# Value products of the sparse attention stage two groups behind the turns, with two result banks and two turn banks

## What is computed

```python
def nsa_cmp_slc(q, q_pos, kc, vc, c_end, ksb, vsb, rel_bias):
    s_c = einsum(q, kc) * scale + head_bias(rel_bias, rel_c)      # compressed keys
    p_c = masked_softmax(s_c, rel_c >= 0);  o_c = p_c @ vc
    imp = p_c.sum(axis=2)                                         # importance of each block
    score = where(valid, imp + where(forced, FORCE_BONUS, 0.0), -1.0)
    _, idx = top_k(score, min(N_SEL, nsb))                        # 16 blocks of 64 keys
    s_s = einsum(q, ks) * scale + bias_s;  o_s = masked_softmax(s_s) @ vs
    return o_c, o_s
# nsa_window: the same over the last 512 keys -> o_w
o = gt[:, :, 0] * o_c + gt[:, :, 1] * o_s + gt[:, :, 2] * o_w
```

## Time and profile before

| | |
|---|---|
| median of 3 runs | 2830.69 us (2830.21 to 2832.34) |
| profiled execution | 2836.41 us |
| its span | 2834.7 us |
| busy PE, DVE, ACT, POOL | 2646.6, 1317.6, 854.3, 701.4 us |
| mean granted TensorE clock | 0.961 |

### The profile page before, as it was taken

The page is one execution under the profiler, slowest core; times in us unless marked ns, Lnnn a source line. Parts: engine busy times, 40 slices in busy tenths (PEclk is TensorE's granted clock), DMA queues, the critical chain, the costliest instruction groups (busy, mean ns, idle before and its releaser), DMA issues. The chain is left out here.

```text
span 2834.7 us, 52982 instructions
## 1 busy us (share of the span) xinstructions
PE 2646.6 (93%) x21938; PEld 2429.6 (86%) x21938; DVE 1317.6 (46%) x2309; ACT 854.3 (30%) x1604; POOL 701.4 (25%) x554
## 2 busy tenths in 40 slices
PE   8999999999789887788879999999999999999997
PEld 8998999989778764455559899988999999999996
DVE  6999989213234356455543353234333323323233
ACT  5333101123123324565552222135221121120222
POOL 2222212222234320211113424301422222222232
PEclk9999999999889887999889999999999999999998
DMA  5122353332476624434316551233111111111112
GB/s 185 48 66 68 99 105 91 92 98 68 139 245 216 214 90 176 133 110 155 115 59 213 150 184 60 75 134 135 47 44 47 50 46 45 45 45 45 45 45 69
DMA packets 149345, 290.33 MB, mean 102 GB/s; under 512 B 28356, under 2 KB 97160, under 8 KB 146354
## 3 DMA queue, kind: packets, MB, share of 16 engines
q1 hardware_dynamic: 137586, 255.49, 28.7%
q0 software_dynamic: 11520, 31.47, 3.5%
HBM read 245.94 MB, written 51.93 MB: 105 GB/s over the span
## 5 line engine op out<-in xcount | busy, mean ns | idle before, releaser
L147 POOL TENSOR_TENSOR mlp_w_low<-mlp_w_raw,mlp_w_high 128x1024 fp32r<-128x1024 f32 x72 | 173.7, 2412 | 649.3 <-ACT mlp_w_high L143 649.3
L371 PE MATMUL in_psum<-x_high,in_w_high 128*128 128x352 f32 x1416 | 266.1, 330 | 21.3 <-DVE x_low L566 11.3
L147 POOL TENSOR_TENSOR in_w_low<-in_w_raw,in_w_high 128x1024 fp32r<-128x1024 f32 x59 | 145.8, 2471 | 546.7 <-ACT in_w_high L143 546.7
L2775 PE MATMUL mlp_psum<-mlp_in,mlp_w_high 128*128 128x352 f32 x1536 | 264.9, 324 | 0.0
L143 ACT ACTIVATE mlp_w_high<-mlp_w_raw 128x1024 fp32r<-128x1024 f32 x72 | 76.4, 1061 | 621.5 <-PE mlp_psum L2775 621.5
L371 PEld LDWEIGHTS in_psum<-x_high,in_w_high 128*128 128x128 f32 x1416 | 236.9, 191 | 29.4 <-issue 15.0
L371 PE MATMUL in_psum<-x_low,in_w_high 128*128 128x352 f32 x1416 | 259.5, 325 | 0.0
L371 PE MATMUL in_psum<-x_high,in_w_low 128*128 128x352 f32 x1416 | 259.0, 324 | 0.0
L2775 PEld LDWEIGHTS mlp_psum<-mlp_in,mlp_w_high 128*128 128x128 f32 x1536 | 251.2, 189 | 0.2
L371 PEld LDWEIGHTS in_psum<-x_low,in_w_high 128*128 128x128 f32 x1416 | 235.4, 190 | 0.0
L371 PEld LDWEIGHTS in_psum<-x_high,in_w_low 128*128 128x128 f32 x1416 | 234.8, 189 | 0.0
(11 more groups left out here) (475 smaller groups left out, 4457.3 us busy)
## 6 DMA issues: line engine op xcount, KB each, us to landing
mlp_w_raw<-in_w_mlp SPq DMA_DIRECT2D x64, 512.0 KB, 3.6
in_w_raw<-in_w_in SPq DMA_DIRECT2D x59, 512.0 KB, 4.2
nsa_ring<-in_cache_slc SPq DMA_DIRECT2D x144, 128.0 KB, 4.0
gdnp_page_ring<-in_cache_cmp POOLq DMA_DIRECT2D x128, 128.0 KB, 4.8
gdnp_page_ring<-in_cache_cmp SPq DMA_DIRECT2D x128, 128.0 KB, 5.0
u_scratch<-stage SPq DMA_DIRECT2D x28, 528.0 KB, 5.3
nsa_ring<-in_cache_slc POOLq DMA_DIRECT2D x112, 128.0 KB, 4.0
aux<-u_scratch SPq DMA_DIRECT2D x24, 528.0 KB, 4.2
```

Of the source, the lines that this page charges most:

```text
L147: self.nc.gpsimd.tensor_tensor(self.low[:, i % 2, 0:k * P], self.raw[:, i % 2, 0:k * P], self.high[:, i % 2, 0:k * P].bitcast(F32), ALU.su ...
L371: return mm(psum[:, e % 2, n, 0:WN], w[:, i % 2, c * P:(c + 1) * P], a[:, c, n * WN:(n + 1) * WN], start=x == 0 and c == 0, stop=x == 2 an ...
L2775: return mm(psum[:, e % 2, n, 0:WN], w[:, i % 2, c * P:(c + 1) * P], a(c)[:, column(n)], start=x == 0 and c == 0, stop=x == 2 and c == CHU ...
```

## The change

Values run two groups behind the turns, and across items: after each turn of group G, PE values all groups up to G-2 (`values_up_to`). Groups are numbered through all items. At i = 6 and behind the last item the remaining ones are valued at once. The results of items alternate between banks 6 and 7 (two regions), and ACT copies a result after the copy of the group two behind the item's last (`keep_result`), but that of item 2 at the end of the item. Turned groups use two PSUM banks; `pt` keeps three slots. DVE's wait for its slot of `s_` asks for the turns of the old item, no longer for its values.

```diff
-    SLOTS, TBANKS, REGIONS, LAG = 4, 3, 4, 3
+    SLOTS, TSLOTS, TBANKS, REGIONS, LAG = 4, 3, 2, 2, 3
...
+    BEHIND = 2
+    place_of_group = [(i, k) for i in range(NI) for k in range(len(groups(i)))]
+    ends_item = {first_group[i + 1] - 1: i for i in range(NI)}
...
-        pt = S("probs_t", [P, TBANKS, 4, P])
+        pt = S("probs_t", [P, TSLOTS, 4, P])
...
-        O_BANK, M0, M1 = 7, 6, 7
-        region = lambda i: ps[:, O_BANK, i % REGIONS * P:(i % REGIONS + 1) * P]
+        O_BANK, M0, M1 = 6, 6, 7
+        region = lambda i: ps[:, O_BANK + i % REGIONS, 0:P]
...
-            def tail(i, step):
-                n = len(groups(i))
-                if step < n:
-                    turn(i, step)
-                if step >= 1:
-                    values(i, step - 1)
+            valued = [0]
+
+            def values_up_to(end):
+                while valued[0] < end:
+                    values(*place_of_group[valued[0]])
+                    valued[0] += 1
...
                 if i == RANKED:
+                    values_up_to(first_group[i - LAG])
                     pe.wait_ge(flags_ready, 1)
...
-                tailing = [(i - LAG, s) for s in range(len(groups(i - LAG)) + 1)] if i >= LAG else []
+                tailing = [(i - LAG, s) for s in range(len(groups(i - LAG)))] if i >= LAG else []
                 for which, (n, k) in merged(scoring, tailing):
-                    (tail if which else score)(n, k)
+                    if which:
+                        turn(n, k)
+                        values_up_to(first_group[n] + k + 1 - BEHIND)
+                    else:
+                        score(n, k)
+            values_up_to(first_group[NI])
...
                     next(exp_parts, None)
+                    if G - BEHIND in ends_item and ends_item[G - BEHIND] != RANKED - LAG - 1:
+                        keep_result(ends_item[G - BEHIND])
+                if i == RANKED - LAG - 1:
+                    keep_result(i)
                 for _ in exp_parts:
                     pass
+
+            def keep_result(i):
+                kind, n, tt = items[i]
                 act.wait_ge(o_mm, i + 1)
...
+            for G in range(first_group[NI], first_group[NI] + BEHIND):
+                if G - BEHIND in ends_item:
+                    keep_result(ends_item[G - BEHIND])
...
                 if i >= SLOTS:
-                    dve.wait_ge(o_mm, i - SLOTS + 1)
+                    dve.wait_ge(pt_mm, first_group[i - SLOTS + 1])
```

More of the change, by code:

```diff
@@ L1741, in values @@
                         for b in range(HB):
-                            last = mm(region(i)[strip(b), :], pt[:, G % TBANKS, j, strip(b)], ring[:, n % SETS, b, j, PAGE:2 * PAGE],
+                            last = mm(region(i)[strip(b), :], pt[:, G % TSLOTS, j, strip(b)], ring[:, n % SETS, b, j, PAGE:2 * PAGE],
                                       start=j == 0, stop=j == 3 and final)
@@ L1745, in values @@
                     x, hf, c = sets[n]
-                    last = mm(region(i), pt[0:NEW, G % TBANKS, 0, :], vn[:, hf, 0 if x == WIN else 1, :], start=False, stop=True)
+                    last = mm(region(i), pt[0:NEW, G % TSLOTS, 0, :], vn[:, hf, 0 if x == WIN else 1, :], start=False, stop=True)
                 else:
@@ L1752, in values @@
                             v = vc[0:w, dims] if x == CMP else vtok[:, 0 if x == SLC else 1, vb, dims]
-                            last = mm(region(i)[dims, :], v, pt[0:w, G % TBANKS, 2 * j + g, :], start=k == 0 and j == 0, stop=x == CMP)
+                            last = mm(region(i)[dims, :], v, pt[0:w, G % TSLOTS, 2 * j + g, :], start=k == 0 and j == 0, stop=x == CMP)
                 last.then_inc(o_mm if final else pv_mm, 1)
-            def tail(i, step):
-                n = len(groups(i))
-                if step < n:
-                    turn(i, step)
-                if step >= 1:
-                    values(i, step - 1)
+            valued = [0]
[3 more added lines that the diff above has]
+                    valued[0] += 1
             for c0, c1, b in ((0, BANK, 0), (BANK, NBIAS, 1)):
@@ L1857, in copies @@
                     act.wait_ge(pt_mm, G + 1)
[L1858 to L1861, removed]
+                    if G >= TSLOTS:
+                        old = max(m for m in range(NI) if first_group[m] <= G - TSLOTS)
+                        finished = G - TSLOTS == first_group[old + 1] - 1
+                        act.wait_ge(*((o_mm, old + 1) if finished else (pv_mm, G - TSLOTS - old + 1)))
                     if kind == SET:
@@ L1865, in copies @@
                         w, cols = (4 * (tt + 1), 2 * P) if group[0][0] == CMP else (P, 2 * P * len(group))
-                    act.activation(pt[0:w, G % TBANKS, :, :].rearrange("p a b -> p (a b)")[:, 0:cols], turn_bank(G)[0:w, 0:cols], ACT.Copy
+                    act.activation(pt[0:w, G % TSLOTS, :, :].rearrange("p a b -> p (a b)")[:, 0:cols], turn_bank(G)[0:w, 0:cols], ACT.Copy
                                    ).then_inc(pt_out, 1)
                     next(exp_parts, None)
+                    if G - BEHIND in ends_item and ends_item[G - BEHIND] != RANKED - LAG - 1:
+                        keep_result(ends_item[G - BEHIND])
+                if i == RANKED - LAG - 1:
+                    keep_result(i)
                 for _ in exp_parts:
                     pass
+            def keep_result(i):
+                kind, n, tt = items[i]
                 act.wait_ge(o_mm, i + 1)
```

## The result

The changed kernel takes 2865.8 us (median of four runs, 2856.7 to 2874.0) against 2831.5 us before (four runs); the ratio is 1.0114, interval 1.0089 to 1.0138. It is slower, 34 us by the medians. The forecast was 2851 us, range 2829 to 2870. The profiled execution took 2867.5 us with a span of 2865.8, 31.1 us above that of before.

What follows compares the result with a forecast made beforehand. PE bounds the sparse stage's item loop, with ring waits, copy waits and half clock. Copies -28, ring +42, clock +6 and banks +1 gave +21, taken as +20.5 on 2830.7: 2851 us, range 2829 to 2870.

Steps and rivals of the forecast that it cites:

- The ring's term: Sparse stage's item loop: later release of ring halves makes PE's waits grow from 15.4 to 57 us, +42 (+34 to +50).
- the clock: Sparse stage's item loop: half-clock episodes rise from ten to fourteen, costing 34 us against 24; +6 (-6 to +15).
- Copies: Sparse stage's item loop: PE's waits for ACT's copies of turned probabilities shrink, 28 us back (20 to 37).
- Score banks: Sparse stage's item loop: PE's 3.3 us of waits for score banks, counted only in the 37 us upper bound given back.
- Two banks of turns, two regions: Sparse stage: turn banks 0 to +2 us, result regions 0, at most +1, drain ahead of block masks +1; +1 summed.
- Rival B: Ring loads keep up, taking under 7 us; waits stay at 15, copies give 28 and clock 8: 2795 us; chance 0.13.
- Rival C: Even: ring waits grow by only 30 us, copy holes close entirely (-34), clock steady: 2826 to 2836 us; chance 0.08.
- Rival D: ACT's order still holds copies back: only 9 us come back, ring waits grow by 50: 2878 us; chance 0.03.

Runs made afterwards that it cites:

- set_at_once: Changed kernel, but PE values everything up to a set right after that set's turns, so the ring's half is released nearly where it was before: 2828.6 us, ratio 0.9986.
- late_results: Changed kernel with PE's old order (values one group behind inside an item), keeping late result copies, two result banks and two turn banks: 2844.1 us, ratio 1.0048.
- keys_first_old_spread: Changed kernel with separate loads of keys (released by scores) and values, scores and turns spread as in the kernel before: 2812.8 us, ratio 0.9937.
- after_short: Changed kernel with only one page of a set loaded each by SP and POOL from set 2 on (14 of 16 loads left out): 2803.0 us, ratio 0.9893.

## Why the prediction was right, step by step

The sign, the mechanism and the range held, and the measured 34 us lie above the 20.5 forecast. The ring's term, the largest, came out within 1 us. Two terms were too small: the clock by some 9 us, and the waits for DVE, which stood in no term and took 13. Copies gave 5 us more than forecast. So it is in part luck that the time lies inside the range: its upper end was made of longer ring waits (+50) and less back at the copies (20), not of a lateness of DVE that the prediction didn't see. One reading of the page was loose, without effect on the sums: PE's row is below 90% in slices 11, 12 and 14 too, ahead of the stage. By the prediction's own steps:

*1. Copy waits.* Forecast 28 us back of 37; measured 32.6. One more value product ahead and no wait for results close nearly all holes, and this is nearer the upper bound. Where the ring is out of the way the change gains only 18 and 15 us; part of the rest goes to DVE, step 4.

*2. Ring waits.* Forecast 57 us in fourteen places, 10 or more at set 4 and over 8 at set 15; measured 56.7 in 13, 13.0 and 8.4. The other counted shortfalls, counted / measured: set 2 2.8/2.7, 3 2.7/2.3, 5 6.5/4.8, 6 4.7/3.8, 8 3.7/1.6, 10 7.5/7.1, 11 4.0/2.1, 12 3.0/2.7, 14 1.9/1.9, 16 6.1/5.1, 17 1.5/1.2. The issue order and one load's length gave a table that the chip followed at every set but set 9, where 1.0 us was counted and none came. Without set 4 the counted shortfalls sum to 54.2 us and the waits to 43.7; that the total met the forecast of 57 is owed to a judgement between 49 and 60, and to set 4. There the prediction named head 2's load ahead on SP but gave it no price, and it costs 3 us in the changed kernel and over 6 in set_at_once.

The cited rule of the Trainium skill ("DMA: Bandwidth & Descriptors", Rules for kernel authors), to issue early and wait late, agrees with the trace: issued later, the same loads cost PE 56.7 us of waits in place of 15.4. The estimate from that page's fit, 6.8 us for a set's load, does not hold here. The page gives the fit for one DMA, and a set is 16 of them: the ring waits of the changed kernel ended 9.1 to 10.3 us behind the release, but for set 4's 13.0. With 26 and 4 us of shortfalls that estimate's sum is +1 and not -1, which changes nothing here.

*3. The clock.* Forecast +6 us with +15 as its bound; measured +17 by the episodes and +14.8 by PE's busy time. The prediction's list has eleven waits over 2.6 us, not twelve, so by its own count thirteen episodes were to come; fifteen came. Eleven of them begin inside a ring wait or less than 2 us behind one, as at 1186.3, and hold 5.6 us of busy PE each, not the 4.8 of before. I should have taken the mean of the episodes behind ring waits: before, there were four (at 1191, 1304, 1393 and 1413), with 6.0 us each. The other four (at 1138.5, 1302.4, 1428.7 and 1490.1; 20.2 us of busy PE) begin in the same way at waits of 1.9 to 3.1 us for DVE, so some 10 us of the clock's loss go with step 4. One of them, and the wait in which it begins:

```profile
1302.40:1305.80 3.40, 3.07 (x11) 1.24 (x12) 2.32 (x18) 0.71 (x2) 0.00 (x0) 0.50 0.57 221
1302.73 2.08 PE L1709 MATMUL nsa_psum<-nsa_k_prompt,nsa_q_heads 64*128 64x512 f32 x4 [3.12 <-DVE nsa_part_max L1998]
```

By the cited rule of the Trainium skill ("TensorE: Matmul & The Clock Gate", Loop structure matters more than you think) the prediction had worked out +15, nearer the measured time than its own +6. That is luck: the episodes behind copy waits, which it would keep, did go with the copy waits (34.1 us to 1.5).

*4. Score banks.* Forecast no cost; measured +10.8 us, and +2.4 for scaled probabilities. With its share of the clock this is the term most mis-sized. The prediction had no term for DVE at all, since PE waited 3.3 us for it before. The score-bank waits stay at 12 to 17 us in every kernel that values two groups behind (14.1, 12.4, 17.1, 15.3, 16.1, 12.0) and at 14.2 with one group across items, with long ring waits or none, and are 3.3 to 6.7 in the five with the old order. DVE in turn waits 53.2 us for exponentials in the changed kernel; before it was:

```profile
DVE nsa_scale L1996 <- ACT nsa_probs L1846: 21.6, 17, 2.5
```

late_results copies its results just as late, has the two banks and the new slot wait of DVE, and has 5.6 us, so none of these alone is the cause, and keys_first_old_spread excludes the shifted scores. It also speaks against DVE's waits for exponentials as the whole cause, since these fell to 26.6 us while PE's waits for DVE stayed. What is left is that values cross the items' ends. One explanation that no run told apart is that PE, rid of its copy waits, only comes sooner to score banks that DVE empties no faster: the five kernels with low score-bank waits hold PE for 22.9 us or more in copy waits, the others for 15.8 or less.

*5. Two banks of turns, two regions.* Forecast 0 to +2 for the turn banks, at most +1 for the regions and +1 for the drain ahead of the masks: measured 0 for the turn banks alone, 0.3 us of region waits in the changed kernel, and at the drain 0.5 us where 1.2 stood before.

Rival B needed a load under 7 us, and after_short is that case: it came out at 2803, where B said 2795. Rival C's reason, that the work between release and score runs slower than its prices, was seen: without set 4 it took some 10 us off the counted waits. But they still grew by 41 us and not by 30, and the clock was not steady. Rival D didn't happen: copy waits didn't stay.

## What to carry to other kernels

When an operation is moved later, list every semaphore that it raises and who refills a buffer on it, and count the work that is left between the refill and its first use. A stall of about 1 us (34 copy waits, 34.1 us) at many items can be cheap beside a load that comes late (13 waits, 56.7 us). Taking PE's small stalls away can also uncover the next engine, here DVE. A buffer whose parts are needed at different times should be refilled in parts, each on its own release. A queue that serves two releases in a fixed order must be sorted again when one of them moves.

## What the runs showed of the hardware

SP needs 3.2 us of its own between a head's loads and the ring's, where the kernel has it read its nine page numbers into registers. This is seen only where SP comes late. In the changed kernel the last bias load of head 2 is issued by 1185.5 and the first ring load at 1188.75, though its release was at 1184.2. The kernel before has the same at set 4: 1184.75, 1187.99 and a release at 1185.58, so the 10.4 us from which the prediction took its load's length already held some of it. Elsewhere it would lie under the wait for the release; it was not timed by itself.

512 page loads of 64 KB in place of 256 of 128 KB left no wait on the loads of cache pages.

Ring waits cost more than themselves: short loads took 46 us of them from the changed kernel, and the time fell by 63. In the loop PE's idle time fell by 38.5 us, since some waits for DVE came instead, and its busy time by 27.6, with 60 us less of it at half clock.

A fall of the clock needs no wait on a DMA: in the kernel before, five of ten half-clock episodes begin inside or less than 2 us behind waits of 1.7 to 2.1 us for a copy by ACT, and after the change four of fifteen follow waits for DVE of 1.9 to 3.1 us. Not every such wait did it: those of 2.03 us at 1141.5 and 2.26 us at 1169.2 in the kernel before were followed by none.
